# Packed masks and a new engine for the masked operands of a delta-rule block inversion

## The chip, the core and the metric

One core of a Trainium2 chip runs the program. The metric is the device time of one execution in microseconds (us). The engines of the core are TensorE (PE for matmuls, PEld for weight loads), VectorE (DVE), ScalarE (ACT), GpSimd (POOL) and SyncE (SP, which here only starts transfers). They run their own instruction streams and meet at semaphores.

## What is computed

One inference step of a hybrid decoder layer: a gated delta-rule mixer beside a latent attention, a cross attention to a memory, and a mixture of 32 experts, for a prompt of 256 tokens and 8 sample sequences of one token each with a past of 2048 tokens. The change lies in the delta rule of the prompt. In the reference it is written in chunks of 64 tokens:

```python
lower = jnp.where(strict, jnp.einsum('bnhcd,bnhsd->bnhcs', kb, kc) * decay, 0.0)
eye = jnp.eye(C, dtype=jnp.float32)
wy = lax.linalg.triangular_solve(eye + lower, jnp.broadcast_to(eye, lower.shape),
                                 left_side=True, lower=True, unit_diagonal=True)
u = jnp.einsum('bnhcs,bnhse->bnhce', wy, vb)
w = jnp.einsum('bnhcs,bnhsd->bnhcd', wy, kb * jnp.exp(gc)[..., None])
```

So for each of 4 heads and 4 chunks a unit lower triangular 64x64 matrix is inverted. All else stays as it is.

## The kernel before

The program is a row of blocks with a barrier of all engines after each. Two of them matter here.

The first block (lines 445 to 1028) projects the inputs, makes the gates, the keys and values, and the prompt's attention. At its end VectorE makes, for t = 0 and 1 (two tiles of 128 tokens, that is two chunks of 64 on top of each other on the partitions), the transposed strictly lower matrices `LT` of four heads, 128 columns a head (line 899), the intra-chunk product `iT` (line 900), the first masked operand `CTc` with `level_part(dve, 0, t)` (line 901) and the start of the inverse, `XTc` = identity - `CTc` (line 903). `LT` is stored 128x128 per head, but only its two 64x64 corners hold a chunk: rows 0 to 63 with columns 0 to 63, rows 64 to 127 with columns 64 to 127. `Xc`, `CTc`, `XTc` and `Yc` hold corners alone, 64 columns a head. A masked operand is therefore made by two VectorE instructions, one a corner (line 435), each on 64 partitions and 256 elements, with a mask of 128 columns a level from the table of constants in `cst`. `LT` and `XT` are slots of one arena, 1024 columns each; `XTc` takes the first 512 columns of `XT`.

The second block (lines 1158 to 1264) doubles the inverted block size in five levels, m = 1 to 5 (`LEVELS` = 6). In a level TensorE multiplies `CTc` with `Xc` for t = 0 and t = 1 (line 1233, which counts `y_made`), ScalarE copies the results to `Yc` (line 1199), TensorE multiplies with `XTc` (lines 1242 and 1243, which count `z_made`), and VectorE subtracts from `Xc` and `XTc` (lines 1176 and 1177, which count `x_ready`). Between these products every engine does steps of the sample sequences' attention over their cached past, `sampled_pe`, `sampled_dve`, `sampled_act` and `sampled_pool`, two a level; lines 1033 to 1077 are TensorE's part, 1095 and 1087 VectorE's, 1107 and 1115 ScalarE's. VectorE makes the masked operand of level 1 as its first instructions of this block, and that of level m+1 as soon as level m's `Y` products have read the old one (it waits for `y_made`, and counts `c_ready`). TensorE waits for `c_ready` from level 2 on.

GpSimd has in this block only the gathers of cached rows: `load_sequence` for slots 1 and 2 at its start, two indirect transfers each (line 412), and later one when a slot comes free. All transfers of weights are started by SP, each when the buffer that it fills is free.

Of the kernel before, what the change touches and what calls it, by code (L numbers as in the profile page):

```python
# [10 lines left out]
ALU = mybir.AluOpType  # L11
# [3 lines left out]
P = 128  # L15
# [6 lines left out]
H = 4  # L22
CHUNK = 64
# [17 lines left out]
LEVELS = 6  # L41


C_ID, C_ONE, C_TRI, C_BLK, C_LVL = 0, 128, 256, 384, 512
C_BEF = C_LVL + LEVELS * P
C_CAUS = C_BEF + P
C_IOTA = C_CAUS + P
C_CH2 = C_IOTA + SLOTS
# [17 lines left out]
def constants():  # L66

    r = np.arange(P)
    row, col = r[:, None], r[None, :]
    c = np.zeros((P, C_ALL), np.float32)  # L70
    c[:, C_ID:C_ID + P] = row == col
    c[:, C_ONE:C_ONE + P] = 1.0
    same = row // CHUNK == col // CHUNK
    c[:, C_TRI:C_TRI + P] = (row <= col) & same
    c[:, C_BLK:C_BLK + P] = same
    for m in range(LEVELS):
        c[:, C_LVL + m * P:C_LVL + (m + 1) * P] = (row < col) & ((row ^ col) >> m == 1)
    c[:, C_BEF:C_BEF + P] = row < col
    c[:, C_CAUS:C_CAUS + P] = np.where(col <= row, 0.0, NEG)
    c[:, C_IOTA:C_IOTA + SLOTS] = 1 + np.arange(SLOTS)[None, :]  # L80
    c[:, C_CH2:C_CH2 + 2] = row // CHUNK == np.arange(2)[None, :]
    for g in range(2):
        c[:, C_SEQ + g * P:C_SEQ + (g + 1) * P] = row == 4 * g + col // 32
    half = ROPE // 2
    freq = (1.0 / (np.float32(10000.0) ** (np.arange(half, dtype=np.float32) / np.float32(half)))).astype(np.float32)
    for t in range(NT):
        pos = (t * P + r if t < 2 else np.full(P, PAST)).astype(np.float32)
        ang = (pos[:, None] * freq[None, :]).astype(np.float32)
        c[:, C_COS + 32 * t:C_COS + 32 * (t + 1)] = np.cos(ang)
        c[:, C_SIN + 32 * t:C_SIN + 32 * (t + 1)] = np.sin(ang)  # L90
    c[:, C_PAGE:C_PAGE + P] = row == col // (P // NPAGE)
    c[:, C_SUB] = r % (P // NPAGE)
    c[:, C_HEAD:C_HEAD + H] = row % 32 == np.arange(H)[None, :]
    sel = np.repeat(np.tile(np.eye(NE, dtype=np.float32), (3, 1)), SLOTS, axis=1)
    return c, sel.astype("bfloat16")


class Chain:
# [5 lines left out]
    def link(self, eng, ins):  # L104
        self.n += 1
        ins.then_inc(self.sem, 1)
        eng.wait_ge(self.sem, self.n)
# [26 lines left out]
def rep1(ap, shape):  # L134

    return ap.unsqueeze(1).broadcast_to(shape)
# [6 lines left out]
def build(nc, x_prompt, x_sample, state_gdn, state_conv, cache_latent, cache_krope, page_table,  # L143
# [22 lines left out]
    cst = keep("cst", [P, C_ALL])  # L166
# [7 lines left out]
    def c_(at, n=P, rows=P):  # L174
        return cst[0:rows, at:at + n]

    ident = c_(C_ID)
    dve_chain, act_chain, pool_chain = (Chain(sem(n, True)) for n in ("dve_steps", "act_steps", "pool_steps"))
# [106 lines left out]
    row = heads.take([P, TOK])  # L285
# [124 lines left out]
    def load_sequence(pool, b):  # L410
        for slots, rows in ((lat_slots, lat_rows), (kr_slots, kr_rows)):
            pool.indirect_dma_start(slots[b % NSLOT].rearrange("p i n -> p (i n)"), None, rows,
                                    bass.IndirectOffsetOnAxis(ap=idx[:, b:b + 1].bitcast(mybir.dt.uint32), axis=0)).then_inc(seq_loaded[b % NSLOT], 16)
# [8 lines left out]
    def own_blocks(whole):  # L422
        return whole.rearrange("p t h n -> p (t h n)")[:, 0:2 * H * CHUNK].rearrange("p (t h n) -> p t h n", t=2, h=H)

    Xc, CTc, XTc, Yc = (own_blocks(whole) for whole in (X, CT, XT, Y))
    HALVES = (slice(0, CHUNK), slice(CHUNK, P))
    for_sample = Arena(arena, AT_SLOTS)
    kz, qz = (keepers.take([P, H, DEC, DEC]) for _ in range(2))
    qk = keepers.take([P, H, DEC])
    delta = for_sample.take([P, DEC, P])  # L430
    def level_part(dve, m, t):

        for half in HALVES:
            mask = cst[half, C_LVL + m * P + half.start:C_LVL + m * P + half.stop]
            last = nc.vector.tensor_tensor(CTc[half, t], LT[half, t, :, half], rep1(mask, [CHUNK, H, CHUNK]), ALU.mult)
        return last

    g, beta = gw[:, 6, :].rearrange("p (t h) -> p t h", h=H), gw[:, 7, :].rearrange("p (t h) -> p t h", h=H)
    state_loaded = sem("state_loaded", True)
# [5 lines left out]
    with nc.Block() as block:  # L445
# [248 lines left out]
        def _(dve):  # L694
            link = lambda ins: dve_chain.link(dve, ins)
# [200 lines left out]
            for t in range(2):  # L896
                dve.wait_ge(g1["products"], t + 1)
                kk, qk = (ps[:, bank, :].rearrange("p (h n) -> p h n", h=H) for bank in KV_BANKS[t])
                link(nc.vector.tensor_tensor(LT[:, t], LT[:, t], kk, ALU.mult))
                nc.vector.tensor_tensor(iT[:, t], decT[:, t], qk, ALU.mult)  # L900
                link(level_part(dve, 0, t))
                for half in HALVES:
                    nc.vector.tensor_tensor(XTc[half, t], rep1(ident[half, half], [CHUNK, H, CHUNK]), CTc[half, t], ALU.subtract)

        @block.scalar
        def _(act):
# [251 lines left out]
    with nc.Block() as block:  # L1158
        @block.vector
        def _(dve):  # L1160
            of_heads = lambda bank, side: ps[:, bank, side * H * CHUNK:(side + 1) * H * CHUNK].rearrange("p (h n) -> p h n", h=H)
            for t in range(2):
                dve_chain.link(dve, level_part(dve, 1, t))
                dve.wait_ge(x_turned, t + 1)
                nc.vector.tensor_copy(Xc[:, t], of_heads(t, 1)).then_inc(x_ready, 1)
            for m in range(1, LEVELS):
                if m + 1 < LEVELS:
                    for t in range(2):
                        dve.wait_ge(y_made, 2 * (m - 1) + t + 1)
                        level_part(dve, m + 1, t).then_inc(c_ready, 1)  # L1170
                for k in level_steps(m, False):
                    sampled_dve(dve, k)
                for t in range(2):
                    dve.wait_ge(z_made, 2 * (m - 1) + t + 1)
                    if m + 1 < LEVELS:
                        nc.vector.tensor_tensor(Xc[:, t], Xc[:, t], of_heads(t, 0), ALU.subtract)
                    nc.vector.tensor_tensor(XTc[:, t], XTc[:, t], of_heads(t, 1), ALU.subtract).then_inc(x_ready, 1)
                for k in level_steps(m, True):
                    sampled_dve(dve, k)
            q_s, k_s = (qkv[:, i * H:(i + 1) * H, SEQ:TOK] for i in range(2))  # L1180
            for padded, x in ((kz, k_s), (qz, q_s)):
                dve_chain.link(dve, nc.vector.memset(padded, 0.0))
                nc.vector.tensor_copy(padded.rearrange("p h b n -> p h (b n)")[:, :, 0:DEC * DEC:DEC + 1], x)
            nc.vector.tensor_tensor(qk, q_s, k_s, ALU.mult)
            for t in range(2):
                dve.wait_ge(uw_made, t + 1)
                nc.vector.tensor_copy(u[:, t], ps[:, t, :].rearrange("p (h n) -> p h n", h=H))
            dve.wait_ge(uw_made, 3)
            for i, half in enumerate(HALVES):
                nc.vector.tensor_copy(wT.rearrange("p t h n -> p (t h) n")[:, :, half], ps[:, 2 + i, :].rearrange("p (m n) -> p m n", m=2 * H))  # L1190
# [17 lines left out]
        @block.gpsimd  # L1208
        def _(pool):
            for b in range(1, NSLOT):  # L1210
                load_sequence(pool, b)
            for k in range(STEP_SCAN):
                sampled_pool(pool, k)

        @block.tensor
        def _(pe):
# [8 lines left out]
                last.then_inc(x_turned, 1)  # L1225
            for m in range(1, LEVELS):
                for t in range(2):
                    if m > 1:
                        pe.wait_ge(c_ready, 2 * (m - 2) + t + 1)
                    pe.wait_ge(x_ready, 2 * (m - 1) + t + 1)  # L1230
                    for h in range(H):
                        for half in HALVES:
                            last = pe.matmul(block_of(t, 0, h, half), CTc[half, t, h, :], Xc[half, t, h, :], start=True, stop=True)
                    last.then_inc(y_made, 1)
                for k in level_steps(m, False):
                    sampled_pe(pe, k)
                for t in range(2):
                    pe.wait_ge(y_moved, 2 * (m - 1) + t + 1)
                    for h in range(H):
                        for half in HALVES:  # L1240
                            if m + 1 < LEVELS:
                                pe.matmul(block_of(t, 0, h, half), XTc[half, t, h, :], Yc[half, t, h, :], start=True, stop=True)
                            last = pe.matmul(block_of(t, 1, h, half), Yc[half, t, h, :], XTc[half, t, h, :], start=True, stop=True)
                    last.then_inc(z_made, 1)
                for k in level_steps(m, True):
                    sampled_pe(pe, k)
# [1475 lines left out]
```

## Time and profile before

| | us |
|---|---|
| median of 3 runs | 1496.4 |
| lowest and highest run | 1494.47, 1496.8 |
| span of the profiled execution, first to last instruction | 1494.2 |

| engine | busy us | share |
|---|---|---|
| PE | 1373.9 | 92% |
| DVE | 460.2 | 31% |
| ACT | 201.1 | 13% |
| POOL | 42.6 | 3% |

The two blocks named above end at about 153.5 and 203.5 us of the span. Register, branch, semaphore and transfer-starting instructions are not counted as busy. In the rows below "L435" is line 435 of the kernel, "<-" between two names reads "written from", "128x512" is partitions by elements, "xN" the number of instructions; "[0.30 <-issue]" says how long the engine sat idle before and what ended that ("issue": nothing that the profile shows). A trailing q (POOLq, PEq, SPq) is an engine's sequencer.

### The profile page before, as it was taken

Reading aid. Unit: us, or ns where it says so; the run is one execution under the profiler, and the core shown is the slowest. Engines: PE = TensorE matmul, PEld = TensorE weight load, DVE = VectorE, ACT = ScalarE, POOL = GpSimd, SP = SyncE. Lnnn points to the kernel's source line nnn. Section 1 sums busy time; section 2 is a strip of 40 time slices with the busy share of each in tenths; the row PEclk is TensorE's granted clock in tenths of the full one; section 3 lists DMA queues with packets and bytes.
Section 4 is the critical chain, followed back from the end, with each engine's and each line's share of the span. In section 5 each row is a group of like instructions: output and inputs, shape, how many; then the busy total and the mean of one; then the engine's idle time right before and its main releaser. Section 6 shows DMA issues by size and latency. Waiting matters only on the chain.

```text
span 1494.2 us, 21159 instructions
## 1 busy us (share of the span) xinstructions
PE 1373.9 (92%) x8579; PEld 694.5 (46%) x8579; DVE 460.2 (31%) x1116; ACT 201.1 (13%) x399; POOL 42.6 (3%) x37
## 2 busy tenths in 40 slices
PE   8999899899998989999999988989989889899896
PEld 7668766555486453333333333333433333333332
DVE  1856643553024252113113112111221131122213
ACT  1053322321012440000000000000000000000002
POOL 0000101000000320000000000000000000000000
PEclk9999999999999989999999999999999999999999
DMA  9111534448365669999999999999999999999996
GB/s 367 39 53 57 199 143 149 184 150 329 141 253 180 225 276 413 389 413 424 426 425 424 428 425 424 427 424 426 425 424 429 423 424 426 424 426 427 424 426 245
DMA packets 96727, 490.73 MB, mean 328 GB/s; under 512 B 9307, under 2 KB 14527, under 8 KB 61626
## 3 DMA queue, kind: packets, MB, share of 16 engines
q1 hardware_dynamic: 94074, 468.89, 76.8%
q0 software_dynamic: 2304, 20.97, 3.6%
q8 instruction: 39, 0.64, 0.2%
q10 hardware_dynamic: 296, 0.11, 0.0%
q14 instruction: 14, 0.11, 0.0%
HBM read 484.01 MB, written 6.04 MB: 328 GB/s over the span
## 4 chain that ended last, share of the span: by engine, by line
PE 40%; DMA 18%; DVE 6%; issue 2%; SPq 1%; ACT 1%; POOL 1%; DVEq 0%
PE ps L2039 17%; DMA arena<-in_w_e 17%; PE ps L2076 14%; PE ps L2032 2%; PE ps L2064 1%; DVE arena L2604 1%; DVE arena L2614 1%; DVE arena L2611 1%; PE ps L2088 1%; DVE arena L2612 1%; SPq L1467 1%; DMA arena<-in_cache_mem_k 1%; PE ps L2104 1%; PE ps L2118 1%; PE ps L2112 0%
## 5 line engine op out<-in xcount | busy, mean ns | idle before, releaser
L2039 PE MATMUL ps<-arena 128*64 128x512 f32 x2048 | 454.3, 595 | 22.1 <-DMA arena<-in_w_e 21.5
L2039 PEld LDWEIGHTS ps<-arena 128*64 128x64 f32 x2048 | 148.9, 137 | 303.5 <-issue 278.5
L2076 PE MATMUL ps<-arena 128*64 128x512 f32 x952 | 214.2, 604 | 2.4 <-ACT arena L2291 2.4
L2076 PEld LDWEIGHTS ps<-arena 128*64 128x64 f32 x952 | 77.9, 141 | 136.1 <-issue 123.3
L2611 DVE TENSOR_SCALAR arena<-ps 128x1024 f32<-128x1024 f32 x15 | 18.4, 1225 | 243.5 <-PE ps L2039 243.5
L2032 PE MATMUL ps<-arena 96*128 96x512 bf16 x96 | 35.3, 488 | 46.0 <-DVE arena L2604 46.0
L2623 DVE COPY arena<-ps 128x512 f32<-128x512 f32 x15 | 10.4, 692 | 216.5 <-PE ps L2076 216.5
L2629 DVE TENSOR_TENSOR res<-res,ps 128x512 f32<-128x512 f32 x60 | 41.3, 688 | 115.9 <-PE ps L2088 115.9
L2025 PEld LDWEIGHTS ps<-arena 128*128 128x128 bf16 x768 | 49.5, 99 | 14.0 <-issue 12.2
L1753 PE MATMUL ps<-arena 128*128 128x512 f32 x128 | 55.8, 594 | 0.0
L2025 PE MATMUL ps<-arena 128*128 128x128 bf16 x768 | 54.0, 222 | 1.7 <-DVE arena L2578 1.7
L2088 PE MATMUL ps<-arena 128*128 128x512 f32 x120 | 55.5, 605 | 0.0
L2289 ACT ACTIVATE arena<-arena 128x1024 f32<-128x1024 f32 x15 | 15.9, 1057 | 293.5 <-DVE arena L2611 293.5
L1107 ACT COPY arena<-ps 128x384 f32<-128x384 f32 x64 | 30.6, 478 | 98.7 <-PE ps L1035 98.1
L2595 DVE TENSOR_SCALAR arena<-cst,arena 128x64 bf16<-128x64 f32 (+1 forms) x90 | 22.2, 247 | 62.2 <-PE ps L2056 62.2
L1095 DVE COPY arena<-ps 128x256 f32<-128x256 f32 x64 | 26.8, 423 | 44.5 <-PE ps L1039 41.0
L2293 ACT COPY arena<-ps 128x512 f32<-128x512 f32 x15 | 8.8, 587 | 218.1 <-PE ps L2076 218.1
L1753 PEld LDWEIGHTS ps<-arena 128*128 128x128 f32 x128 | 24.0, 190 | 29.2 <-issue 29.1
L2088 PEld LDWEIGHTS ps<-arena 128*128 128x128 f32 x120 | 21.6, 189 | 33.7 <-issue 33.7
L2032 PEld LDWEIGHTS ps<-arena 96*128 (+1 forms) x96 | 9.7, 115 | 55.4 <-issue 49.0
L538 PE MATMUL ps<-arena,xnT 128*128 128x392 f32 (+2 forms) x96 | 35.3, 525 | 0.0
L2286 ACT COPY arena<-ps 128x256 f32<-128x256 f32 x15 | 5.6, 373 | 219.6 <-PE ps L2056 219.6
(553 smaller groups left out, 1533.0 us busy)
## 6 DMA issues: line engine op xcount, KB each, us to landing
arena<-in_w_e SPq DMA_DIRECT2D x383, 1024.0 KB, 18.0
arena<-in_w_in SPq DMA_DIRECT2D x8, 1380.0 KB, 17.6
arena<-in_cache_mem_k SPq DMA_DIRECT2D x8, 1024.0 KB, 8.9
arena<-in_w_out SPq DMA_DIRECT2D x2, 2048.0 KB
arena<-in_w_xk SPq DMA_DIRECT2D x1, 4096.0 KB, 15.9
arena<-in_w_xv SPq DMA_DIRECT2D x1, 4096.0 KB, 13.8
arena<-in_w_xq SPq DMA_DIRECT2D x1, 4096.0 KB, 23.2
arena<-in_cache_mem_v SPq DMA_DIRECT2D x1, 4096.0 KB, 16.1
```

The source lines that it names most:

```text
L538: last = pe.matmul(ps[:, bank, 0:b - a], xnT[:, k, cols(t)], win[:, k, CONV + a:CONV + b], start=(k == 0), stop=(k == KD - 1))
L1095: nc.vector.tensor_copy(KT[:, k % 2, p, 3 * P:5 * P], ps[:, key_banks(k, p)[1], 0:2 * P]).then_inc(sa["odd_moved"], 1)
L1107: nc.scalar.copy(KT[:, k % 2, p, 0:3 * P], ps[:, key_banks(k, p)[0], 0:3 * P]).then_inc(sa["even_moved"], 1)
L1753: last = pe.matmul(ps[:, i % 4, :], memT[:, k, cols(t)], w[:, k, n * 512:(n + 1) * 512], start=(k == 0), stop=(k == KD - 1))
L2025: pe.matmul(out, xp[:, t, i, k * P:(k + 1) * P], picked[:, t, :], start=(t == 0 and i == 0), stop=False)
L2032: pe.matmul(ps[:, bank, :], mine, b1[:, a + i * 512:a + (i + 1) * 512], start=True, stop=True)
L2039: last = pe.matmul(ps[64 * x:64 * x + 64, c, :], xe[:, k, 64 * x:64 * x + 64], weights[x][:, c * 512:(c + 1) * 512], start=False, stop=(k ...
L2076: last = pe.matmul(ps[64 * x:64 * x + 64, 4 + c, :], aT[:, k, 64 * x:64 * x + 64], weights[x][:, j * D + c * 512:j * D + (c + 1) * 512], s ...
L2088: pe.matmul(ps[:, COMBINE_BANKS[2 * t + c], :], gT[:, t, :], ye[:, c * 512:(c + 1) * 512], start=True, stop=True).then_inc(lp["combined"], 1)
L2595: last = nc.vector.tensor_scalar(picked[0:q, t, 64 * x:64 * x + 64], io, slot[0:q, t, place], None, ALU.is_equal)
L2611: nc.vector.tensor_scalar(glu[:, :].rearrange("p (c n) -> p c n", c=4), hid[:, :, :, 0], 7.0, None, ALU.min).then_inc(lp["glu"], 1)
L2629: nc.vector.tensor_tensor(a, a, ps[:, COMBINE_BANKS[i], :], ALU.add).then_inc(lp["added"], 1)
```

## The change

The table of constants gets masks of 64 columns a level, whose rows are counted within a chunk, so that one mask serves both corners at once; an identity of the same form (`C_EYE`) is added. The corners of `LT` are no longer kept 128 columns a head: line 899's product is made in two instructions, one a corner, straight into `LTc`, 64 columns a head, in the second 512 columns of `XT`'s slot. `level_part` then is one instruction on 128 partitions and 256 elements instead of two on 64, and so is the start of `XTc`.

In the second block the masked operands of levels 1 to 5 go from VectorE to GpSimd, behind its two `load_sequence` calls and ahead of its sampled steps: ten instructions, those of level 2 and up each behind a wait for `y_made` of the level before. TensorE now waits for `c_ready` at level 1 too.

```diff
 C_ID, C_ONE, C_TRI, C_BLK, C_LVL = 0, 128, 256, 384, 512
-C_BEF = C_LVL + LEVELS * P
+C_EYE = C_LVL + LEVELS * CHUNK
+C_BEF = C_EYE + CHUNK
...
-        c[:, C_LVL + m * P:C_LVL + (m + 1) * P] = (row < col) & ((row ^ col) >> m == 1)
+        own = (row % CHUNK < col[:, 0:CHUNK]) & ((row % CHUNK ^ col[:, 0:CHUNK]) >> m == 1)
+        c[:, C_LVL + m * CHUNK:C_LVL + (m + 1) * CHUNK] = own
+    c[:, C_EYE:C_EYE + CHUNK] = row % CHUNK == col[:, 0:CHUNK]
...
+    LTc = XT.rearrange("p t h n -> p (t h n)")[:, 2 * H * CHUNK:4 * H * CHUNK].rearrange("p (t h n) -> p t h n", t=2, h=H)
...
-    def level_part(dve, m, t):
-
-        for half in HALVES:
-            mask = cst[half, C_LVL + m * P + half.start:C_LVL + m * P + half.stop]
-            last = nc.vector.tensor_tensor(CTc[half, t], LT[half, t, :, half], rep1(mask, [CHUNK, H, CHUNK]), ALU.mult)
-        return last
+    def level_part(eng, m, t):
+
+        return eng.tensor_tensor(CTc[:, t], LTc[:, t], rep1(c_(C_LVL + m * CHUNK, CHUNK), [P, H, CHUNK]), ALU.mult)
...
-                link(nc.vector.tensor_tensor(LT[:, t], LT[:, t], kk, ALU.mult))
+                for half in HALVES:
+                    last = nc.vector.tensor_tensor(LTc[half, t], LT[half, t, :, half], kk[half, :, half], ALU.mult)
+                link(last)
                 nc.vector.tensor_tensor(iT[:, t], decT[:, t], qk, ALU.mult)
-                link(level_part(dve, 0, t))
-                for half in HALVES:
-                    nc.vector.tensor_tensor(XTc[half, t], rep1(ident[half, half], [CHUNK, H, CHUNK]), CTc[half, t], ALU.subtract)
+                link(level_part(nc.vector, 0, t))
+                nc.vector.tensor_tensor(XTc[:, t], rep1(c_(C_EYE, CHUNK), [P, H, CHUNK]), CTc[:, t], ALU.subtract)
...
             for t in range(2):
-                dve_chain.link(dve, level_part(dve, 1, t))
                 dve.wait_ge(x_turned, t + 1)
                 nc.vector.tensor_copy(Xc[:, t], of_heads(t, 1)).then_inc(x_ready, 1)
             for m in range(1, LEVELS):
-                if m + 1 < LEVELS:
-                    for t in range(2):
-                        dve.wait_ge(y_made, 2 * (m - 1) + t + 1)
-                        level_part(dve, m + 1, t).then_inc(c_ready, 1)
...
             for b in range(1, NSLOT):
                 load_sequence(pool, b)
+            for m in range(1, LEVELS):
+                for t in range(2):
+                    if m > 1:
+                        pool.wait_ge(y_made, 2 * (m - 2) + t + 1)
+                    level_part(nc.gpsimd, m, t).then_inc(c_ready, 1)
             for k in range(STEP_SCAN):
                 sampled_pool(pool, k)
...
-                    if m > 1:
-                        pe.wait_ge(c_ready, 2 * (m - 2) + t + 1)
+                    pe.wait_ge(c_ready, 2 * (m - 1) + t + 1)
```

## Rows read from the trace of the kernel before

**Rows 1.** The page: busy time of PE, and the DMA share in 40 slices.

```profile
PE 1373.9 (92%) x8579; PEld 694.5 (46%) x8579; DVE 460.2 (31%) x1116; ACT 201.1 (13%) x399; POOL 42.6 (3%) x37
DMA  9111534448365669999999999999999999999996
```

**Rows 2.** The page: the chain that ended last, by line, shares of the span.

```profile
PE ps L2039 17%; DMA arena<-in_w_e 17%; PE ps L2076 14%; PE ps L2032 2%; PE ps L2064 1%; DVE arena L2604 1%; DVE arena L2614 1%; DVE arena L2611 1%; PE ps L2088 1%; DVE arena L2612 1%; SPq L1467 1%; DMA arena<-in_cache_mem_k 1%; PE ps L2104 1%; PE ps L2118 1%; PE ps L2112 0%
```

**Rows 3.** Waits of SP: who waited, for whom, us in total, times, longest.

```profile
SPq L1463 <- PE ps L2076: 232.2, 59, 13.4
SPq L1467 <- PE ps L2039: 162.5, 44, 6.7
```

**Rows 4.** Waits of PE from 200 to 560 us, the longest.

```profile
PE ps L2104 <- DMA arena<-in_cache_mem_k: 4.9, 2, 3.2
```

**Rows 5.** Waits of PE from 157.5 to 203 us, all of them.

```profile
PE ps L1071 <- ACT res L1115: 2.1, 2, 1.2
PE ps L1233 <- issue: 1.0, 1, 1.0
```

**Rows 6.** The masked products' line: count, shortest/median/longest in ns, first and last start.

```profile
L435 DVE TENSOR_TENSOR arena<-arena,cst x24: 409/420/423, 147.1 to 182.8; 64x256 f32<-64x256 f32 x24
```

**Rows 7.** Timeline of DVE and ACT, end of the first block: start us, us, instruction.

```profile
145.81 0.67 DVE L899 TENSOR_TENSOR arena<-arena,ps 128x512 f32<-128x512 f32 x1
...
147.99 0.85 DVE L903 TENSOR_TENSOR arena<-cst,arena 64x256 f32<-64x256 f32 x2
...
151.06 0.85 DVE L903 TENSOR_TENSOR arena<-cst,arena 64x256 f32<-64x256 f32 x2
...
151.39 0.37 ACT L1009 COPY xnT<-ps 128x256 f32<-128x256 f32 x1 [0.30 <-PE ps L691]
```

**Rows 8.** Timeline of POOL at the second block's start, first and last of four.

```profile
154.24 1.05 POOL L412 DMA_INDIRECT arena<-in_cache_latent,arena  x1 [44.32 <-POOLq L160]
...
158.19 1.04 POOL L412 DMA_INDIRECT arena<-in_cache_krope,arena  x1 [0.30 <-issue]
```

**Rows 9.** Timeline of PE at the second block's start.

```profile
153.62 1.97 PE L1224 MATMUL ps<-cst,arena 64*64 64x64 f32 x32 [2.27 <-PEq L160]
155.33 1.12 PE L1233 MATMUL ps<-arena 64*64 64x64 f32 x16
156.67 0.84 PE L1233 MATMUL ps<-arena 64*64 64x64 f32 x16 [0.22 <-DVE arena L1165]
157.44 0.44 PE L1033 MATMUL ps<-cst,arena 128*128 128x128 f32 x2
```

**Rows 10.** Timeline of POOL and ACT, products at 523 to 547 us and a hand-over.

```profile
523.77 2.13 POOL L2414 TENSOR_TENSOR arena<-arena 128x1024 f32<-128x1024 f32 x1 [6.77 <-ACT arena L2306]
...
544.66 1.15 POOL L2414 TENSOR_TENSOR arena<-arena 128x512 f32<-128x512 f32 x1 [2.27 <-ACT arena L2306]
...
505.38 2.75 ACT L2321 CAST arena<-arena 32x3072 bf16<-32x3072 f32 x1 [6.12 <-POOL arena L2426]
```

**Rows 11.** POOL's first product: the line's instructions (ns), then its row in the timeline.

```profile
L2426 POOLq MODIFY_POOL_CONFIG  x2: 13/13/13, 494.9 to 495.0; - x2
...
499.34 6.00 POOL L2426 TENSOR_TENSOR arena<-arena 96x3072 f32<-96x3072 f32 x1 [4.33 <-ACT arena L2319]
```

**Rows 12.** Windows: PE, PEld, DVE, ACT, POOL busy (x), PEclk, DMA share, GB/s.

```profile
153.60:157.00 3.40, 3.16 (x54) 2.99 (x56) 2.88 (x7) 0.37 (x1) 2.15 (x3) 0.51 0.45 126
157.00:160.50 3.50, 3.50 (x87) 3.26 (x85) 2.68 (x8) 1.33 (x3) 1.93 (x2) 0.99 1.10 332
...
204.90:208.90 4.00, 4.00 (x49) 2.12 (x37) 0.42 (x1) 0.48 (x1) 0.00 (x0) 0.58 0.00 0
```

**Rows 13.** Timeline of PE, the next level's first products.

```profile
162.78 1.15 PE L1233 MATMUL ps<-arena 64*64 64x64 f32 x32
```

**Rows 14.** The gathers' line, issue to landing; the first block's end on POOL (ns).

```profile
DMA to landing us min/median/max: 8.2/8.9/18.5
...
L445 POOLq DRAIN x1: 10373/10373/10373, 107.8 to 107.8; - x1
```

## The prediction

> **What bounds the kernel now.** I read the page first, then the chain that ended last, the waits of SP and PE, and last the timeline of the two blocks that change. The page shows TensorE busy for 92% of the span, and the DMA engines full only from the 16th slice on, that is from about 560 us [rows 1]. The chain says what that means: its long links are the experts' products (L2039, L2076) and the arrival of expert weights (in_w_e, 17%) [rows 2]. So the second half of the run is held by the stream of expert weights. The change lies at 145 to 203 us, ahead of it, so the question is whether a shift there reaches the end. SP starts the expert loads when a buffer is free, and its two longest waits are for TensorE's own products [rows 3]; between 200 and 560 us TensorE's longest wait for a transfer is 4.9 us, on keys that SP starts only in that later block [rows 4]. No load stands ready that could swallow a shift: what is lost or won by 203 us moves the stream's start and so the end, one for one.
>
> Inside the second block TensorE is what runs through. From 157.5 to 203 us it waits 2.1 us for ScalarE's softmax and 1.0 us for nothing that the profile shows, and never for VectorE [rows 5]. The reader should see that the engine which is relieved is not the one that is waited for.
>
> **The sum, part by part.** It is made against the profiled span, 1494.2 us. The median of the runs is 1496.4, 2.2 us more, which I add at the end.
>
> First block. For each t, line 899's one instruction of 0.67 us becomes two on 64 partitions; the 64x256 products of L435 take 0.42 each [rows 6], so 0.84 in place of 0.67. The masked operand goes from two of these to one (-0.42), and so does the start of `XTc`, 0.85 for two [rows 7] (-0.42). That is about -0.67 us for each t, -1.3 us together. VectorE's last instruction ended at 151.06 + 0.85 = 151.91, ScalarE's at 151.39 + 0.37 = 151.76 [rows 7]. The barrier needs both. ScalarE is late next, so 0.15 us is gained and the rest of the 1.3 us is covered.
>
> Levels 2 to 5 of the second block. VectorE loses 16 products of 0.42 us, 6.7 us. Since TensorE waits there for ScalarE alone [rows 5], this is worth nothing. GpSimd has to fill the same slots. Its products cost 2.13 us for 1024 elements and 1.15 for 512 [rows 10], 1.91 ns an element, so 256 take about 1.15 - 0.49 = 0.66 us; the two of a level, 1.3 us. The level's old operand is free when the `Y` products end, at 156.67 + 0.84 = 157.51 in level 1, and the next is read at 162.78 [rows 9, 13]: 5.3 us of cover, the shortest of the four gaps. At nothing, then; if a product took over 2.6 us, the excess would count in each level. The mask is read with a repeated column pattern that no GpSimd row has; as a bound I let it cost as much as 512 elements, 1.15 us.
>
> Level 1, where the price lies. TensorE has not waited for `c_ready` here; now it does, and behind that wait its whole stream stands, then ScalarE and VectorE behind it. On GpSimd the two first products stand behind four gathers: they run one after the other from 154.24 with 0.30 us between, the last until 158.19 + 1.04 = 159.23 [rows 8]. The next instruction starts at 159.53 at the soonest. TensorE began the level's products at 155.33 [rows 9].
>
> Ahead of GpSimd's first product there is something more. In the trace its first TENSOR_TENSOR, at 499.34, has two MODIFY_POOL_CONFIG on its line, at 494.9 and 495.0, and no other instruction of the program has them [rows 11]. They belong to the use of this kind of instruction after the gathers and memsets, so they should move to the new first product. They are 13 ns each themselves; what they set going took from nothing to 4.33 us, because the product started 4.33 us later, but behind an operand of ScalarE that came just then [rows 11]. Bounds: 0 and 4.33 us. I take 4.3, the upper end, since there, in the 14th slice, the DMA engines were some six tenths busy [rows 1] and here they are full (share 1.10 between 157 and 160.5 [rows 12]), so whatever is fetched is not fetched sooner.
>
> A rule of the Trainium skill speaks against the change here. Its page GPSIMD Engine Reference (Instruction dispatch) says that the first call to a freshly loaded kernel pays about 6 us for the load of its code, counted from MODIFY_POOL_CONFIG, with nothing in the profile to show for it, and under Terminology that this code is brought by DMA. The trace allows at most 4.33 us for its one case. By the page's figure the sum would come to an estimated 1507.7 instead of the 1506.1 below.
>
> So: first product 159.53 + 4.33 = 163.86 to 164.52; the hand-over to a waiting engine takes 0.04 us (GpSimd's product ends at 499.34 + 6.00 = 505.34, ScalarE starts at 505.38 [rows 10, 11]); TensorE starts level 1 at 164.56. The second product is there by 165.2, before the first 16 matmuls end. The 32 matmuls take 1.97 us at the low clock, as the 32 of L1224 did [rows 9], and the sampled step starts at 166.53 instead of 157.44: +9.1 us.
>
> The clock. TensorE's granted clock was 0.51, that is 1.2 GHz, from 153.6 to 157.0, behind the idle stretch of the barrier, and full again after 3.4 us of work; behind the next barrier it was 0.58 on the mean for 4.0 us [rows 12]. After the new idle stretch of some 9 us I expect the same 3.4 us at 1.2 GHz. Level 1's products ran at that clock before as well, so they cost no more. The remaining 1.45 us fall on sampled work that ran at 2.4 GHz before, and half of that is lost: +0.7 us, with 0 and (4.0 - 1.97) / 2 = 1.0 as bounds.
>
> Sum: -0.15 + 9.1 + 0.7 = +9.7 us, span 1503.9, and with the 2.2 us around it **1506.1**.
>
> Ends of the unknowns. Lowest: nothing for the configuration, none for the clock, and TensorE's unexplained 1.0 us gone: 9.7 - 4.3 - 0.7 - 1.0 = +3.7, 1500.1. Highest: the configuration stretched as the gathers are when the DMA engines are full, 18.5 us to landing against a median of 8.9 [rows 14], that is 4.33 x 2.1 = 9.1, +4.8; slow products, +0.65; the clock, +0.3: 1511.9. Smaller things with one answer: the table of constants shrinks and is loaded long before it is used; the third gather (slot 3) now stands behind level 5's product, which waits for level 4's products, made before the sampled step that frees the slot, so it isn't late; nor do the waits of GpSimd hold anything else.
>
> **The rivals.** (a) The configuration costs under 2 us, being only 13 ns of rows. Then only the four gathers and one product stand ahead: 160.23 for TensorE's start, +4.8 - 0.15 + 0.7 = +5.3 us, **1501.7**. For it: the one case shows no time that isn't ScalarE's. Against: a gap of 4.33 us can hide all of it. (b) GpSimd goes on only when its gathers have landed. At the first block's end its DRAIN lasted 10.4 us from 107.8, long after the gathers' own rows, and about as long as these take to land [rows 14]; if the configuration needs such a drained engine, the first product waits for the fourth gather, 158.19 + 18.5 = 176.7, and TensorE starts 17.1 us later than reckoned above, +26.8, **1523.2** (1518.9 without the 4.3). Against: the four gathers themselves are started 1.3 us apart [rows 8], none waiting for the one before to land. (c) The other side, not slower: VectorE's masked products are what holds the array. Its place is the four gaps before levels 2 to 5, its price four times 1.7 us of VectorE time, 6.7 us, and it decides once TensorE idles behind VectorE in each of them and the start costs no more than (a). Then 1501.7 - 6.7 = **1495.0**, and below 1493.4 only if level 1's start loses 1.6 us less than in (a) as well. Against it stand the waits of TensorE, which name VectorE nowhere from 157.5 on [rows 5]. (d) The shift happens but is taken back before the end, because a load was waiting anyway: no change, 1496.2. Against: the waits of SP [rows 3].
>
> **How the numbers follow.** The forecast (a configuration of 2 us up to 9) has 0.50, (a) 0.31, (b) 0.11, (d) 0.05, (c) 0.03. A measurement of this kernel can tell about 0.2%, 3.0 us, from no change. Slower by more: forecast, (a) and (b), 0.92. Within: (d) and a third of (c), 0.06. Faster: the rest of (c), 0.02. The predicted time is the forecast's, 1506.1. The range takes in the forecast's bounds and (a): from 1500.0 to 1513.0, which holds 0.81 and leaves out (b), (c) and (d).
>
> **What would show it.** Right: on TensorE's timeline L1233's first products start about 9 us later than 155.33, released by GpSimd, with an idle stretch behind L1224; on GpSimd's, MODIFY_POOL_CONFIG on the line of the masked product, then ten products of about 0.66 us; no wait of TensorE for GpSimd in levels 2 to 5; the clock low again for some 3 us after the restart; the first block's barrier released by ScalarE; the expert stream's first loads and the end later by the same amount. Wrong: GpSimd's first product directly behind the fourth gather (a), or only at 177 us (b); waits of TensorE for GpSimd in later levels, if the repeated mask is slow; an end that moved less than the start of level 2, if something downstream had slack.

## The result and the profile after

The changed kernel takes 1499.46 us (median of 22 runs, 1495.14 to 1505.12) against 1495.84 us for the kernel before (22 runs, 1490.48 to 1502.59), a ratio of 1.0024 with the 95% interval [1.0013, 1.0036]: 3.6 us slower, 1.9 to 5.4. A second timing, beside the experiments, gave 1502.14 against 1494.54, 1.0053 [1.0035, 1.0070], which is 5.2 to 10.5 us. The two intervals hardly touch; together they put the loss near 5 us. The prediction was slower by 9.7 us, with 1500.0 us as its lower end: the sign was right, the size too large, and the first median fell just under the range.

The profiled execution of the changed kernel spans 1495.2 us, shorter than its median, so its span alone says little: that of before was 1494.2. The places in the trace say more. From the page, busy times and DMA share:

```profile
PE 1379.0 (92%) x8579; PEld 693.9 (46%) x8579; DVE 450.7 (30%) x1094; ACT 201.1 (13%) x399; POOL 49.3 (3%) x47
DMA  8120534448365679999999999999999999999995
```

VectorE lost 9.5 us and GpSimd gained 6.7 [rows 1]: the work moved as it was meant to. The stream of expert weights still fills the second half.

TensorE's timeline at the start of the second block (start, us, instruction, idle before and its releaser). Line 1226 was 1224, line 1234 was 1233, line 1035 was 1033:

```profile
150.62 1.15 PE L1226 MATMUL ps<-cst,arena 64*64 64x64 f32 x32 [2.11 <-PEq L163]
156.80 1.97 PE L1234 MATMUL ps<-arena 64*64 64x64 f32 x32 [5.03 <-POOL arena L437]
158.70 0.69 PE L1035 MATMUL ps<-cst,arena 128*128 128x128 f32 x2
```

Here is the loss: 5.03 us of TensorE waiting for GpSimd, behind the turning of `X`. Level 1 begins 6.18 us after the block's first matmul; before it was 1.71 [rows 9]. GpSimd's timeline in the same stretch, where line 415 issues the gathers:

```profile
151.24 0.94 POOL L415 DMA_INDIRECT arena<-in_cache_latent,arena  x1 [42.91 <-POOLq L163]
...
154.97 0.94 POOL L415 DMA_INDIRECT arena<-in_cache_krope,arena  x1 [0.30 <-issue]
156.02 1.41 POOL L437 TENSOR_TENSOR arena<-arena,cst 128x256 f32<-128x256 f32 x2
158.01 1.58 POOL L437 TENSOR_TENSOR arena<-arena,cst 128x256 f32<-128x256 f32 x2 [0.58 <-PE ps L1234]
```

The first product starts 0.11 us behind the fourth gather (154.97 + 0.94 = 155.91). All instructions of line 437, the masked products (ns shortest/median/longest, first and last start):

```profile
L437 POOL TENSOR_TENSOR arena<-arena,cst x10: 726/729/741, 156.0 to 184.2; 128x256 f32<-128x256 f32 x10
L437 DVE TENSOR_TENSOR arena<-arena,cst x2: 418/418/419, 145.7 to 148.0; 128x256 f32<-128x256 f32 x2
L437 POOLq MODIFY_POOL_CONFIG  x2: 32/32/32, 155.9 to 155.9; - x2
```

The pair of configuration instructions moved here, as predicted, but sits in that 0.11 us. And the product that carried the pair before no longer has it, yet starts with the same idle time ahead of it as in rows 11:

```profile
500.97 6.00 POOL L2427 TENSOR_TENSOR arena<-arena 96x3072 f32<-96x3072 f32 x1 [4.33 <-ACT arena L2320]
```

The idle time is the same with the pair ahead of it and without it: it was the wait for ScalarE's operand, both times. TensorE's waits from 150 to 206 us, all of them (who, for whom, us, times, longest):

```profile
PE ps L1234 <- POOL arena L437: 5.0, 1, 5.0
PE ps L1226 <- PEq L163: 2.1, 1, 2.1
PE ps L1073 <- ACT res L1117: 2.1, 2, 1.2
PE ps L1035 <- PEq L1160: 1.6, 1, 1.6
```

One wait for GpSimd, in level 1; none in levels 2 to 5. The clock in windows (PE, PEld, DVE, ACT, POOL busy, then the granted clock, DMA share, GB/s):

```profile
152.80:156.80 4.00, 0.00 (x1) 0.00 (x1) 0.00 (x0) 0.00 (x0) 3.28 (x5) 0.51 1.06 314
156.80:163.10 6.30, 6.30 (x80) 5.85 (x82) 0.86 (x3) 1.70 (x4) 2.08 (x3) 0.50 0.98 389
163.10:180.00 16.90, 16.90 (x369) 14.54 (x366) 8.06 (x21) 5.79 (x13) 2.83 (x4) 1.00 0.55 213
```

The granted clock was at 1.2 GHz for 10.2 us, from inside TensorE's wait until 6.3 us after the restart, against 3.4 us in rows 12.

Does the shift reach the end? The links of the chain with the first products of the experts, in the kernel before, the changed kernel, and a second profile of the changed kernel:

```profile
555.96 10.52 PE ps L2039 x48
```

```profile
557.90 10.52 PE ps L2040 x48
```

```profile
563.01 10.52 PE ps L2040 x48
```

At the second block's last matmul (line 1259, now 1260) the changed profiles stood 2.0 and 5.4 us behind before's, at the experts' first products 1.9 and 7.1, at the span's end 1.0 and 7.6. No load swallows the shift: on the means of the five profiles of these two kernels the changed one is 3.7 us behind at the block's last matmul and 4.0 us at the span's end. The steps of up to 1.7 us between differ from one execution to the next, and they go with the clock: from the block's last matmul to the experts' first products the fourteen profiles of this document's runs take 349.6 to 358.9 us, the three under 352 us with 17 to 24 us of it at 1.2 GHz, the three over 357 us with 37.5. One profile's span therefore can't show a loss of 5 us.

**Where the 4.5 us of the profiles come from.** Three profiles of the changed kernel and two of before, all read from the timelines ("before, again" is the run b2_before_again, "changed, 2nd" and "3rd" are a2_after_again and r0_changed, below); the tail runs from VectorE's line 899 (901 now) to block 2's first matmul, and VectorE's and ScalarE's ends count from the same start.

| us | before | before, again | changed | changed, 2nd | changed, 3rd | mean difference |
|---|---|---|---|---|---|---|
| VectorE's end | 6.11 | 6.11 | 4.63 | 4.63 | 4.63 | -1.48 |
| ScalarE's end | 5.95 | 5.06 | 4.70 | 6.08 | 6.19 | |
| tail of the first block | 7.81 | 7.82 | 6.39 | 7.77 | 7.89 | -0.47 |
| to level 1's first product | 1.71 | 1.37 | 6.18 | 6.17 | 6.16 | +4.63 |
| level 1 to level 2 | 7.45 | 8.29 | 9.24 | 8.38 | 8.45 | +0.82 |
| level 2 to the block's last matmul | 39.19 | 38.65 | 37.91 | 38.98 | 38.35 | -0.51 |

The sum is +4.5 us, inside the first timing's interval and just under the second's. VectorE's and ScalarE's ends are not terms of it, since they lie within the tail. Of the four terms only the start differs by far more than the profiles of one kernel do among themselves; the other terms are differences of means over two and three profiles.

### The profile page after: what moved, and what is told of

Same layout as the page of the kernel before. It is cut to its first block, busy times and chain, and to the rows that moved or that the text cites. A ratio compares the mean times of both kernels' runs of the same rounds, so it can differ in the third digit from the quotient of the medians.

```text
span 1495.2 us, 21147 instructions
## 1 busy us (share of the span) xinstructions
PE 1379.0 (92%) x8579; PEld 693.9 (46%) x8579; DVE 450.7 (30%) x1094; ACT 201.1 (13%) x399; POOL 49.3 (3%) x47
## 4 chain that ended last, share of the span: by engine, by line
PE 42%; DMA 16%; DVE 6%; issue 2%; SPq 1%; ACT 1%; POOL 1%; DVEq 0%
PE ps L2040 19%; DMA arena<-in_w_e 15%; PE ps L2077 14%; PE ps L2033 2%; PE ps L2065 2%; PE ps L2089 1%; DVE arena L2605 1%; DVE arena L2615 1%; DVE arena L2612 1%; DVE arena L2613 1%; DMA arena<-in_cache_mem_k 1%; PE ps L2119 1%; PE ps L2105 1%; SPq L1468 1%; PE ps L2113 0%
## 5 line engine op out<-in xcount | busy, mean ns | idle before, releaser
L2033 PE MATMUL ps<-arena 96*128 96x512 bf16 x96 | 38.7, 529 | 46.1 <-DVE arena L2605 46.1
```

The source lines that it names most:

```text
L2033: pe.matmul(ps[:, bank, :], mine, b1[:, a + i * 512:a + (i + 1) * 512], start=True, stop=True)
```

## The experiments

All are edits of the changed kernel. Ratios are to the kernel before, run beside them.

**Level 1 back on VectorE.** Only levels 2 to 5 stay on GpSimd.

```diff
-            for m in range(1, LEVELS):
+            for m in range(2, LEVELS):
                 for t in range(2):
-                    if m > 1:
-                        pool.wait_ge(y_made, 2 * (m - 2) + t + 1)
+                    pool.wait_ge(y_made, 2 * (m - 2) + t + 1)
                     level_part(nc.gpsimd, m, t).then_inc(c_ready, 1)
...
             for t in range(2):
+                level_part(nc.vector, 1, t).then_inc(c_ready, 1)
                 dve.wait_ge(x_turned, t + 1)
```

> The changed kernel with level 1's two masked products made by VectorE again (packed, one instruction each, ahead of its copies of Xc); levels 2 to 5 stay on GpSimd. Theory P (place in the queue): all the loss of the change is that level 1's products stand behind four gathers, 4.5 us of idle TensorE and then some 2 us at the low clock; the packing gains 1 to 1.5 us at the first block's end. Then TensorE idles no more than 0.3 us between L1226 and level 1's products, the clock is low for at most 3.4 us behind the barrier, block start to level 2's first product takes 9.0 to 9.3 us (before 9.16, changed 15.42), and the time is 1 to 2.5 us below before. Rival S (sharing): the loss comes from GpSimd working beside VectorE in all levels, or from TensorE's wait for it in each; then levels 2 to 5 (level 2's first product to the block's last matmul) take 1 us or more longer than before's 39.2, and the time stays above before.

Measured: 1495.46 us, ratio 0.9997 [0.9978, 1.0016]. TensorE's timeline:

```profile
154.08 1.71 PE L1226 MATMUL ps<-cst,arena 64*64 64x64 f32 x32 [2.10 <-PEq L163]
155.54 1.97 PE L1234 MATMUL ps<-arena 64*64 64x64 f32 x32
```

Level 1 starts 1.46 us after the block's first matmul, and from 150 to 206 us TensorE waits for GpSimd nowhere. So the wait belongs to level 1 alone, and the rival fell: from level 2 to the block's last matmul it takes 38.2 us, no more than before's 39.2. The time was expected 1 to 2.5 us below before's and is not; the tail of the first block is 7.80 us long in this profile, so the packing's gain didn't arrive in it. Nor does this time show that the eight products of levels 2 to 5 are free on GpSimd, since the packing counts in it too: the packing alone, timed beside it (below), is 1.9 us lower.

**Level 1's products ahead of the gathers**, on GpSimd.

```diff
+            for t in range(2):
+                level_part(nc.gpsimd, 1, t).then_inc(c_ready, 1)
             for b in range(1, NSLOT):
                 load_sequence(pool, b)
-            for m in range(1, LEVELS):
+            for m in range(2, LEVELS):
...
```

> The changed kernel with level 1's two products on GpSimd ahead of its four gathers instead of behind them. Theory P: GpSimd starts at about 0.6 us after the block's start, the products are there at 1.4 and 2.1 us, TensorE's level 1 begins at 1.7 as before, with no idle stretch and no low clock beyond that behind the barrier; block start to level 2's first product 9.0 to 9.4 us; time 1 to 2.5 us below before. The gathers start 1.4 us later and are not waited for. Rival L (load of code): the two MODIFY_POOL_CONFIG are cheap in the changed kernel only because something was ready by then; as the first instructions of the block they cost up to 4.33 us, level 1 starts up to 4.5 us late and the time is within 1 us of the changed kernel's.

Measured: 1496.76 us, 1.0007 [0.9986, 1.0028]. Its GpSimd and TensorE timelines:

```profile
154.02 1.41 POOL L437 TENSOR_TENSOR arena<-arena,cst 128x256 f32<-128x256 f32 x2 [42.61 <-POOLq L163]
155.58 0.97 POOL L415 DMA_INDIRECT arena<-in_cache_latent,arena  x1
```

```profile
153.95 1.15 PE L1227 MATMUL ps<-cst,arena 64*64 64x64 f32 x32 [2.11 <-PEq L163]
155.24 1.15 PE L1235 MATMUL ps<-arena 64*64 64x64 f32 x32
```

Its configuration pair, from the line's instructions (columns as above):

```profile
L437 POOLq MODIFY_POOL_CONFIG  x2: 11/11/11, 153.9 to 153.9; - x2
```

The product is GpSimd's first work in the block here, with the pair right ahead of it, and starts 0.07 us after TensorE's first matmul. So the pair costs nothing that shows without gathers to hide it, too, and the rival, a load of code that costs up to 4.33 us, fell. TensorE doesn't wait. For this wait the engine was no obstacle; the place in its queue was. Here too 1 to 2.5 us below before's were expected, and the time is not below. Once more:

> Level 1's GpSimd products ahead of the gathers, once more, to narrow its interval. Theory (the order behind the gathers is the whole loss): no loss of the start, level 1's first product 1.3 us after the block's start, VectorE's tail in the first block 1.5 us shorter, so between the time of before and 1.5 us below it: 0.999 to 1.000. Rival (the products on GpSimd cost something of their own, by the gathers that are now 1.4 us later or in levels 2 to 5): 1.001 or more.

Measured: 1496.40 us, 1.0012 [0.9995, 1.0029]; level 1 again starts 1.29 us after the block's first matmul. That is 5.7 us below the changed kernel, timed beside it (1502.14). Against before, the median lies on the rival's side, 1.001 or more, and the interval holds both.

**The packing alone**, all products on VectorE as before.

```diff
-            for m in range(1, LEVELS):
-                for t in range(2):
-                    if m > 1:
-                        pool.wait_ge(y_made, 2 * (m - 2) + t + 1)
-                    level_part(nc.gpsimd, m, t).then_inc(c_ready, 1)
...
+                dve_chain.link(dve, level_part(nc.vector, 1, t))
                 dve.wait_ge(x_turned, t + 1)
...
+                if m + 1 < LEVELS:
+                    for t in range(2):
+                        dve.wait_ge(y_made, 2 * (m - 1) + t + 1)
+                        level_part(nc.vector, m + 1, t).then_inc(c_ready, 1)
...
-                    pe.wait_ge(c_ready, 2 * (m - 1) + t + 1)
+                    if m > 1:
+                        pe.wait_ge(c_ready, 2 * (m - 2) + t + 1)
```

> Packing alone: the table, LTc and one instruction for each masked product as in the changed kernel, but all products on VectorE at the places of before, none on GpSimd. Theory P: the first block's end gains 1 to 1.5 us (from line 899's product to the barrier 4.7 us instead of 6.1), block start to level 2's first product stays at 9.2 us, levels 2 to 5 stay within 0.3 us of 39.2 apart from TensorE's 1.0 us that nothing explains; time 1 to 2.5 us below before. Rival C (cover): ScalarE's last copy ends the first block anyway, as the prediction had it; then the gain is 0.15 us, and the time is within 0.5 us of before.

Measured: 1493.61 us, 0.9983 [0.9965, 1.0002]. Once more:

> The packed tables with all products on VectorE, once more, to narrow its interval. Theory (the packing takes 1.5 us from VectorE's tail in the first block, of which 0 to 1.4 us arrive, by how long ScalarE's copies last; levels 2 to 5 are hidden): 0.9990 to 1.0000. Rival (VectorE's 6.7 us less in levels 2 to 5 reach the path): 0.9955 to 0.998. The run before gave 0.9983 with [0.9965, 1.0002], which lies between.

Measured: 1492.81 us, 0.9988 [0.9967, 1.0008]. In both sets it has the lowest median, 1.6 and 1.7 us under before's, and both intervals reach 1, so a gain over before is likely but not shown. VectorE's end in the first block's tail is 4.63 us in place of 6.11, and the tail is 6.83 and 6.86 us in place of 7.81. If one version is to be kept, it is this one.

**The array kept at work during the wait.** 36 matmuls of 128x128 f32 on the identity, whose results nobody reads, ahead of level 1.

```diff
                 last.then_inc(x_turned, 1)
+            for _ in range(36):
+                pe.matmul(ps[:, 4, 0:P], ident, ident, start=True, stop=True)
             for m in range(1, LEVELS):
```

> The changed kernel with 36 matmuls of the identity with itself (128x128, into a PSUM bank that is free then) between L1226 and level 1's products, so that TensorE works through the time in which it waits for GpSimd; their result is used nowhere. Theory P with a clock share: the products still come 6.1 us after the block's start, but the granted clock is at its full level by level 1's first sampled step or stays up, so that block start to level 2's first product falls from 15.4 to between 13.2 and 14.0 us, and the time is 1 to 2 us below the changed kernel's. Rival N (no clock share): the 2 us between the start of level 1 and that of level 2 are not the clock's; then it stays at 15.2 to 15.6 us.

Measured: 1499.36 us, 1.0029 [1.0006, 1.0052]. The matmuls took 9.33 us and overran the wait, so level 1 starts 10.88 us after the block's first matmul; the total can't be read. From level 1 to level 2 it is 6.42 us, against 8.69 on the mean in the changed kernel. With sixteen in place of 36:

> The changed kernel with 16 matmuls of 128x128 f32 on the identity, whose results nobody reads, between the turning of X and the wait for level 1's products; the 36 of the run before took 9.33 us and overran the wait by about 4.7 us. Sixteen take 4 to 5 us and end about where the wait ends, so level 1's first product starts 6.2 to 6.6 us after the block's first matmul, as in the changed kernel. Theory (the idle array brings a second loss, by the clock): from level 1's first to level 2's first product 6.4 to 7.5 us instead of 9.24, so 1.8 to 2.8 us of the loss is gone, and the time is 1497 to 1498 us. Rival (the clock of these 10 us is not owed to the idle array): 9.2 us there again, and 1499.5 us.

Measured: 1498.11 us, 1.0022 [1.0007, 1.0038]. TensorE's timeline and the window up to level 1 (columns as above; the profile has two instructions for each of the sixteen):

```profile
154.48 1.15 PE L1226 MATMUL ps<-cst,arena 64*64 64x64 f32 x32 [2.11 <-PEq L163]
155.56 3.84 PE L1229 MATMUL ps<-cst 128*128 128x128 f32 x32
160.65 0.56 PE L1236 MATMUL ps<-arena 64*64 64x64 f32 x12 [1.25 <-POOL arena L437]
```

```profile
154.50:160.65 6.15, 4.90 (x65) 4.64 (x65) 0.85 (x2) 0.00 (x0) 4.53 (x6) 1.00 0.78 227
```

Now the wait is the same, 6.17 us to level 1, but the clock stays at 2.4 GHz, and level 1 to level 2 takes 6.63 us. So the stretch at 1.2 GHz is owed to the idle array, in the trace. In time it is worth at most some 2 us (8.69 - 6.63), which the timing doesn't show: 1.0022 stands beside the changed kernel's 1.0024 and 1.0053.

**Two gathers ahead instead of four.** Level 1's products between the second and the third sequence's gathers.

```diff
-            for b in range(1, NSLOT):
-                load_sequence(pool, b)
+            load_sequence(pool, 1)
+            for t in range(2):
+                level_part(nc.gpsimd, 1, t).then_inc(c_ready, 1)
+            load_sequence(pool, 2)
...
```

> The changed kernel with level 1's two GpSimd products issued between the gathers of the second and of the third sequence: two gathers stand ahead of them instead of four. If the start is lost to the issue time of the gathers (1.24 us each, 0.94 us and a gap of 0.30), the first product of level 1 comes 2.5 us earlier: its start after block 2's first matmul falls from 6.18 us to about 3.7, against 1.71 before the change. On the clock: if the stretch at 1.2 GHz inside the block is owed to the array's idle time, it is shorter than the changed kernel's 10.3 us, and level 2's first product stands between 9.2 us (before) and 15.4 us (changed) behind the block's start, near 11.5. The whole then loses about half of what the changed kernel loses, 1497 to 1498 us. If two gathers or four make no difference (a fixed price on GpSimd's first product in the block), the first product stays at about 6.2 us and the time at 1499.

Measured: 1499.14 us, 1.0031 [1.0018, 1.0044]. TensorE's timeline:

```profile
151.84 1.83 PE L1227 MATMUL ps<-cst,arena 64*64 64x64 f32 x32 [2.10 <-PEq L163]
155.53 1.97 PE L1235 MATMUL ps<-arena 64*64 64x64 f32 x32 [1.86 <-POOL arena L437]
```

The start follows the count of gathers: 1.29 us with none ahead, 3.69 with two, 6.18 with four, about 1.2 us each. The time did not follow by half in this run. Once more:

> Level 1's products between the two sequences' gathers, once more: its first timing was 1.0031 with [1.0018, 1.0044], where half of the changed kernel's loss, 1.0015, was expected from its profile (first product at 3.69 us after the block's start). Theory (the loss goes with the wait): 1.0010 to 1.0020. Rival (something else in this order costs 2 us more, such as the second sequence's gathers 1.5 us later): 1.0030 again, and then the third sequence's rows land late enough to be waited for by the attention matmuls.

Measured: 1498.27 us, 1.0018 [1.0003, 1.0033], start again at 3.68 us. That is 3.9 us below the changed kernel, timed beside it (1502.14). Against before, the two medians are 4.8 and 3.7 us higher, not far below the changed kernel's 3.6 and 7.6. No wait of TensorE for the gathered rows up to 460 us appears, so the rival's cause isn't there; that the loss goes with the wait is shown for the start, and not for the last microsecond or two of the whole.

**The two kernels profiled again**, and the changed kernel timed again.

> The kernel before once more, for its profile alone. Theory (the tail of the first block is set by ScalarE's copies, and its length differs by where a stretch at 1.2 GHz falls, not by the change): the time from the first packed-away operation of that tail to block 2's first matmul is 7.8 us if 6.8 us of the tail run at 1.2 GHz, and 6.8 us if 3.4 us do, as in the kernels with packed masks. Rival (the change shortens the tail by over 1 us): 7.8 us whatever the clock.

> The changed kernel once more, for its profile alone. Theory: the wait of TensorE for GpSimd's first product of block 2 is there again, 5.0 us, and level 1's first product starts 6.2 us after the block's first matmul; the tail of the first block is 7.8 us long if it has 6.8 us at 1.2 GHz, 6.4 to 6.8 us if it has 3.4 us; the 1.0 us gap in level 3, which the changed kernel's first profile lacks, may be there or not. Rival (the changed kernel's tail is shorter by its own doing): 6.4 us with either clock.

> The changed kernel, timed beside the three that follow. From the profiles so far (changed twice, before twice; means): block 2's start loses 4.6 us, the clock up to level 2 0.9 us, levels 2 to 5 gain 0.5 us, and the first block's tail gains 0 us where 6.8 us of it run at 1.2 GHz and 1.4 us where 3.4 us do. That is 3.6 to 5.0 us in all, a ratio of 1.0024 to 1.0033. If the losses of the block are partly taken back later, 1.0010 or less.

The last VectorE and ScalarE rows of the first block, first in the second profile of the kernel before, then in that of the changed kernel:

```profile
150.69 0.85 DVE L903 TENSOR_TENSOR arena<-cst,arena 64x256 f32<-64x256 f32 x2
...
150.11 0.37 ACT L1009 COPY xnT<-ps 128x256 f32<-128x256 f32 x1 [0.30 <-PE ps L691]
```

```profile
150.32 0.42 DVE L905 TENSOR_TENSOR arena<-cst,arena 128x256 f32<-128x256 f32 x1
...
151.81 0.37 ACT L1011 COPY xnT<-ps 128x256 f32<-128x256 f32 x1 [0.30 <-PE ps L692]
```

In this profile of before VectorE ends last, at 151.54 against ScalarE's 150.48; in the changed kernel ScalarE ends last, at 152.18 against 150.74. The expectation that the tail's length goes by the clock alone was wrong for the kernel before: here the stretch at 1.2 GHz around the tail's beginning was 3.4 us long (144.6 to 148.0) in place of 6.8 (143.4 to 150.2 in the first profile), and yet the tail took 7.82 us, because VectorE's 6.11 us set it. The rival, a gain by the change whatever the clock, fell too: where that stretch is 6.8 us long the changed tail takes 7.77 and 7.89 us, where it is 3.4 us long 6.39, and 6.83 in the packed kernel. All twelve profiles with packed masks go this way, six with 6.4 to 6.9 us and six with 7.6 to 7.9, and in all fourteen the block's first matmul comes 1.7 us behind the later of VectorE's and ScalarE's ends. Both have their part: VectorE's work is 1.48 us shorter always, and how much of it arrives, 0 to 1.4 us, depends on how late ScalarE's copies are, which follow TensorE's matmuls and their clock. The wait of level 1 was there in all three profiles (5.0, 4.4 and 4.5 us), and the timing is the second one named at the top: 1.0053 is above the 1.0024 to 1.0033 that the profiles had let expect, and its interval begins at 1.0035. The 3.1 us between its 7.6 and the table's 4.5 are in none of the table's terms.

## Why the prediction was wrong in size

**The configuration: the step that failed.** I took 4.33 us between the pair's rows and the product in rows 11 for its price, at the upper end of bounds of 0 and 4.33. It was the wait for ScalarE's operand, as the row itself said. The changed kernel pays 0.11 us at most, all that lies between gather and product. By the rival's sum, +5.3 us, the time would be 1501.7; the two timings gave +3.6 and +7.6 (1502.14 - 1494.54), the profiles' table +4.5. Rival (a) happened; I had given it 0.31. The argument that the fetch would not come sooner when the DMA engines are full was about a fetch that no row showed. From the last gather's end to the product, with the pair between them, pass 0.11 us. The rule of the Trainium skill that I weighed (GPSIMD Engine Reference, Instruction dispatch), some 6 us for the first call to a freshly loaded kernel, is therefore not seen here; no row tells whether this pair loads code at all, and for the time the measurement decides.

**The gathers: right.** The first product was put at 159.53 us and TensorE at 160.23 without the configuration, 6.61 us after the block's first matmul; measured 6.16 to 6.18 in three profiles. Of the 0.4 us between, 0.3 are the gathers, 0.94 us each where the first and the last took 1.05 and 1.04 [rows 8], and 0.2 the gap ahead of the product, 0.11 us in place of 0.30; the product itself is 0.07 longer than reckoned.

**The clock: right in size, by another way.** Predicted +0.7 us with 3.4 us at 1.2 GHz after the restart; the stretch was 10.2 us long in all three profiles, but 4.0 us of it (in the first) passed while the array had nothing to do, and part of the rest was work that ran at 1.2 GHz before as well. Level 1 to level 2 lost 0.82 us on the mean.

**The first block: right for one profile, taken for all.** VectorE's saving was put at 1.3 us and is 1.48: the two corner products take 0.84 us in place of 0.67, and the other two steps 0.42 in place of 0.85. That ScalarE is late next and leaves 0.15 us was true of the profile that I had, in which a stretch of 6.8 us at 1.2 GHz held ScalarE up. I gave this term no bound; it needed one of 0 to -1.4 us, and with it the range would have held the first median. Another 0.6 us of the distance is the base: the forecast stood on a median of three runs, 1496.4, and the 22 runs gave 1495.84.

**Levels 2 to 5: right.** GpSimd's product takes 0.73 us (predicted 0.66, bound 1.15), no wait of TensorE for it, VectorE's loss of work worth nothing. The stretch was 0.5 us shorter on the mean. In part this is the gap without a releaser, 1.0 us in rows 5, that comes and goes: 0.5 us in before's second profile, none, 0.8 and 0.2 in the changed ones, 1.0 with the products first. It belongs to no edit that I can name.

**Rivals (b), (c) and (d)** fell: the first product didn't wait for the gathers to land, which takes 8.1 us at least after issue; VectorE never held the array; the experts' first products moved with the block. For (d) I had misread rows 4: its 4.9 us are two waits together, the longest is 3.2. That changes no term of the sum.

**Open.** By its profile, the kernel with the products first should gain about what the packing alone gains: its tails are 6.83 and 6.81 us and its second block 47.3 and 47.2 us, against 47.2 and 47.7 for the packing alone. Its timings are 1.6 and 1.9 us above before's instead, with intervals that reach 1, and 3.2 and 3.6 us above the packing alone, timed beside it; with level 1 back on VectorE it is 1.9 us. So some 1.9 to 3.6 us by these medians go with the products on GpSimd although TensorE waits for none of them, and they may be part of the changed kernel's loss as well. The profiles show no wait that accounts for them. The mean granted clock of the timed runs was 0.960 in both sets with the products first, 0.966 and 0.964 with the packing alone, but 0.965 with level 1 back on VectorE; within each kernel the runs with a lower clock tend to be the longer ones. Whether the edit has a part in that is not shown. The engine change with the masks left unpacked wasn't tried.

## What to carry to other kernels

A move to an idle engine is priced at the place in that engine's queue: the busy share of GpSimd was 3%, and yet the four gathers ahead of its first product cost 4.6 us; with the product put first, or that one left on VectorE, this wait was gone. Where a change has two halves, each is to be timed beside the other half alone: beside before, the gain of the packing hides what the other half may cost. An idle time that the profile puts down to a named operand is not a price for something else that happens to lie in it. And which engine is late next at a barrier is to be read as a range when the engines behind it follow a clock that shifts from one execution to the next.

## What the runs showed of the hardware

The pair of MODIFY_POOL_CONFIG ahead of GpSimd's first TENSOR_TENSOR costs no visible time: 0.11 us lie between the last gather and the product, and as the block's first work the product starts with the block. On VectorE a product of 128x256 takes 0.42 us, as long as one of 64x256 [rows 6], so half the partitions save nothing; on GpSimd the same product takes 0.73 us. With TensorE idle for 5.0 us came a stretch of 10.2 us at 1.2 GHz, 6.3 us of it under work; with 3.84 us of matmuls in the wait there was none. And where such a stretch fell on the end of the first block, ScalarE, which copies what TensorE makes, ended up to 1.5 us later (4.70 and 6.19 us after the same start).
